# Routing tile by tile inside the output stage of a fused diffusion step

## What is computed

```python
    return merged @ P['w_out'][l], (k, v)                 # end of _mixing
    ...
    x = x + g1[:, None] * mix
    h2 = _rmsnorm(x, P['norm_ffn'][l]) * (1.0 + sc2[:, None]) + sh2[:, None]
    x = x + g2[:, None] * _moe(h2, P, l)
    ...
    gl = (x @ P['w_route_group'][l] + P['b_route_group'][l])          # _moe: 4 groups
    g_prob, g_idx = lax.top_k(jax.nn.softmax(gl, axis=-1), 1)
    el = (jnp.einsum('td,gde->tge', x, P['w_route_exp'][l]) + P['b_route_exp'][l])   # 4 x 8 experts
    e_prob, e_idx = lax.top_k(jax.nn.softmax(el_sel, axis=-1), MOE_TOP_K)            # 2 of 8
```

## Time and profile before

| | us |
|---|---|
| median of 3 runs | 1176.29 (1175.31 to 1176.36) |
| the profiled execution's own time | 1177.98 |
| its span, first to last instruction | 1176.3 |
| TensorE busy | 1039.6 (88%) |
| VectorE busy | 451.5 (38%) |
| ScalarE busy | 215.8 (18%) |
| GpSimd busy | 231.9 (20%) |

### The profile page before, as it was taken

The page is one execution under the profiler, slowest core; times in us unless marked ns, Lnnn a source line. Parts: engine busy times, 40 slices in busy tenths (PEclk is TensorE's granted clock), DMA queues, the critical chain, the costliest instruction groups (busy, mean ns, idle before and its releaser), DMA issues.

```text
span 1176.3 us, 13722 instructions
## 1 busy us (share of the span) xinstructions
PE 1039.6 (88%) x5215; PEld 627.6 (53%) x5215; DVE 451.5 (38%) x1081; ACT 215.8 (18%) x388; POOL 231.9 (20%) x285
## 2 busy tenths in 40 slices
PE   4999999999999999999998999999369986967950
PEld 2567757776566666656655555455345543434520
DVE  4655674143754644744651000132503111101118
ACT  4110001000333333333300000110111110100104
POOL 3040000100770011111112211022112622212214
PEclk9999999999999999999999999999569998989985
DMA  9931220333342332233234711112699999999934
GB/s 311 361 94 36 72 72 1 117 98 108 92 124 65 122 102 89 73 126 94 79 115 165 253 36 36 36 72 80 270 402 395 362 374 407 406 406 405 375 129 175
DMA packets 101153, 209.75 MB, mean 178 GB/s; under 512 B 8984, under 2 KB 64614, under 8 KB 100960
## 3 DMA queue, kind: packets, MB, share of 16 engines
q1 hardware_dynamic: 87984, 179.18, 42.6%
q0 software_dynamic: 13072, 29.67, 7.2%
q10 hardware_dynamic: 32, 0.01, 0.0%
HBM read 197.77 MB, written 18.72 MB: 184 GB/s over the span
## 4 chain that ended last, share of the span: by engine, by line
PE 80%; DMA 8%; SPq 4%; DVE 4%; issue 3%; ACT 1%; POOL 0%; POOLq 0%; DVEq 0%
PE pair L1687 24%; PE pair L1694 13%; PE pair L1686 6%; PE pair L1911 6%; PE pair L1987 5%; PE pair L1690 4%; DMA dft_region<-in_w_e_up 4%; PE pair L1833 3%; PE pair L2004 3%; SPq L650 3%; PE pair L1897 2%; PE pair L2016 2%; DMA hyena_region<-in_w_e_up 2%; PE pair L1810 2%; PE pair L1866 1%
## 5 line engine op out<-in xcount | busy, mean ns | idle before, releaser
L1687 PE MATMUL pair<-hT_region,ring_region 128*128 128x512 f32 x544 | 280.5, 597 | 0.0
L1686 PEld LDWEIGHTS pair<-hT_region,ring_region 128*128 128x128 f32 x544 | 102.4, 192 | 122.7 <-issue 121.3
L1686 PE MATMUL pair<-hT_region,ring_region 128*128 128x128 f32 x544 | 107.2, 279 | 1.8 <-DVE hT_region L1386 1.5
L827 POOL TENSOR_TENSOR dft_region<-dft_region,padded_region 128x640 f32<-128x640 f32 x24 | 36.9, 1538 | 344.9 <-DVE padded_region L1313 344.9
L1687 PEld LDWEIGHTS pair<-hT_region,ring_region 128*128 128x128 f32 x544 | 83.5, 194 | 0.0
L1313 DVE TENSOR_TENSOR padded_region<-pair,padded_region 128x640 f32<-128x640 f32 x24 | 19.8, 825 | 142.3 <-PE pair L1897 99.1
L1911 PE MATMUL pair<-ring_region,dft_region 128*128 128x512 f32 x160 | 71.3, 605 | 2.6 <-issue 2.6
L1627 DVE TENSOR_TENSOR mixer_region<-pair,mixer_region 128x128 f32<-128x128 f32 x34 | 9.9, 291 | 159.3 <-ACT mixer_region L1063 159.3
L1987 PE MATMUL pair<-ring_region,padded_region 128*64 128x256 f32 x608 | 69.8, 382 | 0.8 <-DMA ring_region<-in_w_e_up 0.8
L852 POOL DMA_INDIRECT moe_pairs<-padded_region,bias_region x34 | 34.2, 1005 | 179.6 <-DVE padded_region L1639 175.2
L1034 ACT ACTIVATE padded_region<-pair,colv 128x640 f32<-128x640 f32 x32 | 25.4, 795 | 232.4 <-PE pair L1687 232.4
(11 more groups left out here) (372 smaller groups left out, 1628.2 us busy)
## 6 DMA issues: line engine op xcount, KB each, us to landing
ring_region<-in_w_ada SPq DMA_DIRECT2D x24, 1024.0 KB, 7.5
ring_region<-in_w_gate SPq DMA_DIRECT2D x16, 1024.0 KB, 5.6
ring_region<-in_w_in SPq DMA_DIRECT2D x13, 1024.0 KB, 5.8
ring_region<-in_w_e_gate SPq DMA_DIRECT2D x12, 1024.0 KB, 12.1
ring_region<-in_w_e_up SPq DMA_DIRECT2D x12, 1024.0 KB, 19.3
ring_region<-in_w_e_down SPq DMA_DIRECT2D x24, 512.0 KB, 16.2
hT_region<-in_w_e_gate SPq DMA_DIRECT2D x7, 1024.0 KB, 10.9
hT_region<-in_w_e_up SPq DMA_DIRECT2D x7, 1024.0 KB, 18.9
```

The costliest lines, as they stand in the source:

```text
L827: pool.tensor_tensor(merged[:, dj, :], merged[:, dj, :], gtmp, ALU.add).then_inc(merged_add, 1)
L1686: mm(ps_[0:m, W0:W0 + TC], lhsT, rhs[:, 0:TC], start=start, stop=stop)
L1687: return mm(ps_[0:m, W0 + TC:1024], lhsT, rhs[:, TC:T], start=start, stop=stop)
```

## The change

Each `out` step is cut into two half steps, `oa` and `ob`, one of 512 columns each. What is turned is no longer the normalised rows but the raw residual rows `x1`, in two half steps `ha` and `hb`, each right behind the half that it turns. The scale (1 + sc2) times the norm's weights is folded into two scaled copies of the router weights, the shift into a row of 36 sums (`router_products` on VectorE within branch 3, and a new TensorE step `shift` after the branch step (3, 5)). The normalising factor is applied to the router's result. `route(t)` now picks group and experts for one tile, `lists(t)` the places of one tile. Lists of tiles 0 to 3 are set up in a step `early`, and only tile 4's part in `blocks`. Weights and probabilities of the experts are computed after the expert list is out. SyncE's first expert loads now wait for `("ob", 4)`.

Diff, cut to its core:

```diff
     for t in range(NT):
-        s += [("out", t)]
-        if t >= 1:
-            s += [("hT", t - 1)]
-        if t >= 2:
-            s += [("route", t - 2)]
-    s += [("hT", NT - 1), ("route", NT - 2), ("route", NT - 1)]
-    s += [("count",), ("pos",), ("ids",), ("blocks",), ("perm",)]
+        s += [("oa", t)]
+        if t:
+            s += [("hb", t - 1), ("route", t - 1)]
+        s += [("ha", t), ("ob", t)]
+        if t:
+            s += [("pos", t - 1)]
+    s += [("hb", NT - 1), ("route", NT - 1), ("early",), ("count",), ("pos", NT - 1), ("ids",), ("blocks",), ("perm",)]
...
-            computed(sp, ("out", NT - 1))
+            computed(sp, ("ob", NT - 1))
             for e in range(FIXED):
                 load_expert(e, RANKS.index(e))
...
+                elif k == "oa":
                     t = st[1]
...
+                    act.wait_ge(x1_done, 2 * t + 1)
+                    own.link(act.activation(junk[:, 0:HD2], x1[:, t, 0:HD2], ACT.Square, accum_out=ssq_first[:, t:t + 1]))
+                    own.put(act.activation(ssq_part[:, t:t + 1], ssq_first[:, t:t + 1], ACT.Identity, bias=c_("eps"),
+                                           scale=1.0 / D))
...
+                elif k in ("ha", "hb"):
+                    t, k0 = st[1], 4 * int(k == "hb")
                     computed(act, st)
...
+                    frees(act.activation(hT[:, k0:k0 + 4, P * t:P * (t + 1)],
+                                         ps(st)[:, 0:HD2].rearrange("p (k t) -> p k t", k=4), ACT.Copy), st)
...
+            def route(t):
...
+                computed(dve, st)
+                frees(stt(lg[:, t, :], ps(st)[:, 0:36], rstd[:, one], shifted[:, min(t, 1), :], ALU.mult, ALU.add), st)
...
+                first_max(gl, r5[0][:, one], c_("gid"), gx[0][:, t, :], group)
+                link(tt(m32[:, t], el, group.unsqueeze(2).to_broadcast([P, NG, NE]), ALU.mult))
+                link(dve.tensor_reduce(ex[0][:, t, :], m32[:, t].rearrange("p g e -> p e g"), AX.X, ALU.add))
+                first_max(ex[0][:, t, :], r5[1][:, one], c_("eid"), ex[4][:, t, :], ex[1][:, t, :])
+                link(stt(ex[3][:, t, :], ex[1][:, t, :], -3e38, ex[0][:, t, :], ALU.mult, ALU.add))
+                first_max(ex[3][:, t, :], r5[2][:, one], c_("eid"), ex[4][:, t, :], ex[2][:, t, :])
...
+                tt(m32[:, t], sel[:, 0, t], sel[:, 1, t], ALU.add).then_inc(mask_done, 1)
...
+                elif k in ("oa", "ob"):
+                    t, h = st[1], int(k == "ob")
+                    kind, half = min(t, 1), slice(HD2 * h, HD2 * (h + 1))
...
+                    frees(tt(tmp, ps(st)[:, 0:HD2], rowb[:, 2 + kind, half], ALU.mult), st)
                     drained(dve, st)
...
+                    tt(x1[:, t, half], x1[:, t, half], tmp, ALU.add).then_inc(x1_done, 1)
...
+                elif k in ("ha", "hb"):
+                    t, half = st[1], int(k == "hb")
+                    pe.wait_ge(x1_done, 2 * t + half + 1)
+                    for i in range(4):
+                        kt = 4 * half + i
+                        ins = turn(p_[:, P * i:P * (i + 1)], x1[:, t, P * kt:P * (kt + 1)])
                 elif k == "route":
                     t = st[1]
-                    drained(pe, ("hT", t))
-                    pe.wait_ge(route_in, 16 * 7)
+                    drained(pe, ("shift",))
                     for kt in range(KD):
-                        ins = mm(p_[:, 0:36], hT[:, kt, P * t:P * (t + 1)], wroute[:, kt, :], start=(kt == 0),
+                        if kt % 4 == 0:
+                            drained(pe, ("hb" if kt else "ha", t))
+                        ins = mm(p_[:, 0:36], hT[:, kt, P * t:P * (t + 1)], wscaled[:, min(t, 1), kt, :], start=(kt == 0),
                                  stop=(kt == KD - 1))
```

More of the change, by code:

```diff
@@ L138, in constants @@
     put("pair", np.stack([s * T + t * P + i for s in range(2) for t in range(NT)], 1))
+    put("pairoff", np.stack([s * T + t * P + i for s in range(2) for t in range(NT)], 1) - 2.0 * NPAIR)
     win = np.array([[2, 8], [4, 16]])[i // 64]
@@ L1231, in combine, with router_products @@
                 drained(dve, st)
+            def router_products():
+                mv = mod[:, :].rearrange("p (i m) -> p i m", m=KD)
+                dve.wait_ge(route_in, 16 * 7)
+                for kind in range(2):
+                    put(tt(wscaled[:, kind], wroute, mv[:, 4 + kind, :].unsqueeze(2).to_broadcast([P, KD, 36]), ALU.mult))
+                    put(tt(products[:, kind], wroute.rearrange("p k n -> p n k"),
+                           mv[:, 6 + kind, :].unsqueeze(1).to_broadcast([P, 36, KD]), ALU.mult))
+                own.wait()
+                dve.tensor_reduce(shift_sums, products.rearrange("p i n k -> p (i n) k"), AX.X, ALU.add).then_inc(shift_ready, 1)
@@ new lines, in lists @@
+            def lists(t):
+                st = ("pos", t)
+                computed(dve, st)
+                of_tile = sel[:, :, t].rearrange("p s g e -> p s (g e)")
+                frees(tt(ranked[:, 0:2, :], of_tile, ps(st)[:, 0:EXPERTS].unsqueeze(1).to_broadcast([P, 2, EXPERTS]),
+                         ALU.mult), st)
+                drained(dve, st)
+                link(dve.tensor_reduce(rankf.rearrange("p (s t) -> p s t", t=NT)[:, :, t], ranked[:, 0:2, :], AX.X, ALU.add))
+                for s in range(2):
+                    n = NT * s + t
+                    put(ts(atplace[:, n, :], c_("place"), rankf[:, n:n + 1], None, ALU.is_equal))
+                    put(ts(idsel[:, n, :], of_tile[:, s, :], c_("pairoff")[:, n:n + 1], None, ALU.mult))
+                own.wait()
+                dve.sem_inc(places_done, 1)
@@ L1457, in _ @@
                     frees(dve.tensor_copy(junk[0:64, 0:P], ps(st)[0:64, 0:P]), st)
-                elif k == "out":
-                    t = st[1]
-                    kind = 0 if t == 0 else 1
+                elif k == "shift":
                     computed(dve, st)
-                    if t == 0:
+                    for kind in range(2):
+                        ins = tt(shifted[:, kind, :], ps(st)[:, 36 * kind:36 * (kind + 1)], rbias, ALU.add)
+                        if kind == 0:
+                            put(ins)
+                    own.wait()
+                    frees(ins, st)
+                elif k in ("oa", "ob"):
+                    t, h = st[1], int(k == "ob")
+                    kind, half = min(t, 1), slice(HD2 * h, HD2 * (h + 1))
+                    computed(dve, st)
+                    if t == 0 and h == 0:
@@ new lines, in _ @@
+                    dve.wait_ge(x1_done, 2 * t + h + 1)
+                    if (k, t) == ("ob", 0):
+                        normal_rows(0)
+                elif k == "route":
+                    route(st[1])
+                elif k == "pos":
+                    if st[1] == 0:
+                        put(dve.memset(idxT[:, 2 * P:4 * P], 0.0))
+                    lists(st[1])
+                    if st[1] < NT - 1:
+                        normal_rows(st[1] + 1)
+                elif k == "early":
@@ L1902, in _ @@
                     ins = turn(p_[0:64, 0:P], mod[:, 0:64])
-                elif k == "out":
-                    t = st[1]
+                elif k == "shift":
+                    pe.wait_ge(shift_ready, 1)
+                    ins = mm(p_[:, 0:72], c_("ones"), shift_sums, start=True, stop=True)
+                elif k in ("oa", "ob"):
+                    t, half = st[1], int(k == "ob")
                     if t == 0:
```

231 lines of the change are left out of this document (105 added, 126 removed).

## The result

The changed kernel takes 1191.94 us (median of 4 runs, 1190.43 to 1193.28) against 1176.32 for the kernel before, run beside it: a ratio of 1.0133, 95% interval 1.0119 to 1.0147. It is slower by 15.6 us. The forecast was 1189.3, within 1180 to 1195.

A forecast was written before the change was run, and what follows sets the result against it. TensorE bounds the output stage, the weight stream the expert stage. Delays of 6.0 + 1.6 + 7.9 + 6.8 = 22.3 us less 9.3 idle stream give +13.0: 1191.0 profiled, median 1189.3 us, range 1180 to 1195.

The forecast's parts named there:

- Work moved ahead: Output stage, TensorE: extra transposes, routing and `pos` steps before the end of `ob` 4 cost 6.0 us.
- `ha` 0: Output stage, TensorE: the first transposing half step waits once for VectorE's rows of `oa` 0, 1.6 us.
- Second half of `route`: Output stage, TensorE: waits for ScalarE's copy of `hb`, 2.0 us in each of four tiles, 7.9 us in all.
- The clock: Output stage, TensorE: one clock fall per tile after the waits, 4 x 1.7 = 6.8 us; bounds 0 and 13.6.
- rows at 788 and 1018: Profile of the kernel before: clock stayed at 1.00 around 2.58 us of transposes and routing and after a 2.14 us wait.
- End of `ob` 4: End of the output stage, where the weight stream starts: 22.3 us later than `out` 4 ended, near 843.3.
- List at 11.5 us behind it: After `ob` 4: expert list cast at about 11.5 us, within the 21.3 us that the fixed loads last.
- Idle stream: Expert stage: the DMA engines' 9.3 us standstill between fixed loads and the next load goes, saving 9.3 us, no more.
- two effects behind it at zero: Expert stage: pair starting at half clock (0 to 1.7 us) and a little DMA time regained; both put at zero.
- Rival 3: Expert stage: the first gather, not the stream, sets the time; -9.0 us, 1167.3, chance 0.08.
- Rival 1: Output stage: the clock stays up, all else as forecast; +6.2 us, 1182.5, chance 0.18.
- Rival 2: Output stage: second half of `route` does not wait and clock stays up; -1.7 us, 1174.6, chance 0.05.

The follow-up runs named there:

- e1: Changed kernel with ScalarE's sum of squares of a tile's first half moved behind the copies of `hb` and `ha`: 1177.34 us, ratio 1.0004 to the kernel before.
- e2: Changed kernel plus two unused 128x512 matmuls between the halves of `route` 0 to 3: 1187.06 us, ratio 1.0076 to the kernel before.
- e3: Changed kernel plus 14 linked, unused VectorE additions ahead of the expert list: 1193.55 us, ratio 1.0132 to the kernel before.
- e4: Changed kernel plus 42 linked, unused VectorE additions ahead of the expert list: 1202.83 us, ratio 1.0208 to the kernel before.
- e7: Changed kernel with 2 MB of expert 1 loaded already in the output stage, after the last branch step: 1184.54 us, ratio 1.0066 to the kernel before.
- e10: Changed kernel, steps reordered so half a tile of matmuls covers each result, plus nine unused matmuls before the pair of experts: 1171.78 us, ratio 0.9964.
- e11: Changed kernel, steps reordered for cover, ScalarE's copies first, 2 MB of expert 1 loaded early, six unused matmuls before the expert pair: 1169.34 us, ratio 0.9939.

## Why the prediction was right

The mechanism held in each step; that the terms add up so closely is in part luck (last point). In the order of the sum:

- *Work moved ahead, 6.0 us.* The output stage grew from 76.8 us (744.21 to 821.04) to 100.9 (743.28 to 844.16), by 24.1. Less the waits and clock falls below, 6.7 us are left for it; it was not measured by itself.
- *`ha` 0, 1.6 us.* Measured 1.60.
- *Second half of `route`, 2.0 us each, 7.9 in all.* Measured 1.95 and three times 1.82: 7.4. The chain counted (rows added, sum of squares, root, copy) is the one that releases it; e1 removed it by order alone.
- *The clock, 4 x 1.7 = 6.8 us.* It fell in all four tiles. Tiles 2 to 4 cost 8.73 - 7.03 = 1.7 each. In tile 1 it fell before the second half of `route`, which took 1.92 instead of 1.08: 0.84 there, 0.46 in the transposes and 1.96 in the half tile, 3.3 in all, the upper bound given for one. Sum 8.4. The prediction chose this against rows at 788 and 1018 that spoke for a clock that stays up. The Trainium skill, "TensorE: Matmul & The Clock Gate", section "A second HAM failure mode: psum-queue depth-cycling", tells of a TensorE that idles for moments between groups of matmuls and swings between its two clocks. This trace agrees: four falls of four, after idle times of 1.82 to 1.95 us. e2, with the idle time filled and all else kept, has none.
- *End of `ob` 4, 843.3.* Measured 844.16. The stage grew by 1.8 us more than the 22.3 forecast, but had begun 0.9 us earlier.
- *List at 11.5 us behind it, with 21.3 to spare.* Measured 13.6, mostly because one small instruction took 2.05 us instead of 0.22 (below). Nothing hangs on it, as e3 shows.
- *Idle stream, -9.3.* From first to last load it was 284.7 us before and 274.5 now: -10.2. The prediction put two effects behind it at zero, and both are there. The pair of experts began at half clock, the stream fell to a share of 0.76 over 896 to 900, and up to the loads behind the pair (52.1 us after the first, 60.3 before) only 8.3 us were won. Between there and 961 us another 1.6 came back.
- *The result.* Sum +13.0, measured +12.8 between the two profiled executions. So close a match is luck: the misses cancel (+0.7 for the work, -0.5 for the waits, +1.6 for the clock, -0.9 for the earlier start, -0.9 for the stream). The median was forecast 1.7 us below the profiled execution; after the change it is 1.1 above. These 2.8 us, less the 0.2 above, are the 2.6 by which the forecast is short of the median. By the ratio and its interval the change costs 14.0 to 17.3 us, more than the sum; one traced execution of each kernel does not show which term is short by the difference.

Rival 3 (the gather sets the pace) is refuted by e3 and e4. Rival 1 (the clock stays up) was put 6.8 us below the forecast; e2, which makes it true, is 6.7 us below the changed kernel by the ratios, 8.3 by the output stage of the traces. Rival 2 (no wait and no fall) was put 1.7 us below the kernel before; e1, which makes it true, is 0.5 above (-0.8 to +1.8).

## What to carry to other kernels

An intermediate result that an in-order engine hands back to TensorE wants a copy that is not queued behind something that waits; before cutting a step in halves, look at what stands ahead of the copy on the other engine. A wait of 2 us between groups of matmuls can cost as much again in clock; here the wait's absence (e1) or matmuls in it (e2) saved that. Where a weight stream is the limit, only its start, its idle time and the moments at which buffers come free count: a shorter chain behind it is worth what the stream stood idle and no more.

## What the runs showed of the hardware

- A VectorE instruction of 128x4 elements with two inputs in SBUF took 2.05 us (e3, e4 and e7 too, 2.03 in e1, 1.75 in e2) instead of 0.22 while GpSimd's addition of 128x1024 ran, and ended within 0.02 us of it (849.00 + 2.05 against 848.69 + 2.34). A reduction with one input, started during the same addition, took its usual 0.16. The Trainium skill, "SBUF — State Buffer", section "Who interferes with whom", says that a VectorE instruction with two SBUF inputs and a GpSimd instruction that reads SBUF exclude each other; the trace agrees.
- In the first output half tile e1 (745.92, after the same 2.57 us of idle time) took 7.10 us where the changed kernel took 8.80: the same TensorE code at the same place can keep the clock in one execution and lose it in another. The traces of e10 and e11 kept it too; the other ten lost it.
- Matmuls that kept TensorE at work up to the weights' arrival kept the clock at 1.00 (e10); with 2.48 us left idle it was lost (e11).
